# Summing expert rows into x on chip, spreading gate tiles, and moving a state copy in a hybrid decoder step

## The reference, cut to what matters

```python
x = x + (g_a * (y_a @ w_br_a) + g_b * (y_b @ w_br_b)) @ w_out     # RWKV-7 branch y_a, sparse attention branch y_b, gates g_a, g_b
x = x + moe_ffn(rms_norm(x, norm_ffn), ...)                       # top 4 of 32 experts per token
y = rms_norm(x, norm_final)

# moe_ffn, for every (token, expert) pair that the router chose
u   = h[token] @ w_up[e] + b_up[e]                                # w_up (32, 1024, 2048)
out = (min(u1, 7) * sigmoid(1.702 * u1) * (clip(u2, -7, 7) + 1)) @ w_down[e] + b_down[e]   # w_down (32, 1024, 1024)
result[token] += softmax_weight[token, e] * out
# and one of the outputs: new_win_kv_sample = the sample window state (8, 512, 2, 2, 64), moved on by one token
```

## Time and profile before

| what | value |
|---|---|
| median of the runs | 1611.16 us (1606.93 to 1612.17, 3 runs) |
| the profiled execution, its own time | 1601.41 us |
| its span, first to last instruction | 1599.6 us |
| mean granted PE clock | 0.952 |
| PE busy | 1341.8 us (84%) |
| DVE, ACT, POOL busy | 365.2, 201.3, 140.0 us |
| DMA, mean over the span | 488.81 MB, 306 GB/s |
| compress, attend_prompt, attend_samples begin | about 207, 293, 416 us |
| route, first_tiles, finish begin | about 533, 571, 1566 us |

### The profile page before, as it was taken

How to read it: one execution, slowest core, us unless ns; L and a number is a source line. 1 busy time by engine, 2 the same in 40 slices (tenths; PEclk the granted TensorE clock), 3 DMA queues, 4 the chain that set the end, 5 groups by cost and what they waited for, 6 DMA issues and landing times. The chain is left out here.

```text
span 1599.6 us, 21367 instructions
## 1 busy us (share of the span) xinstructions
PE 1341.8 (84%) x8262; PEld 665.5 (42%) x8263; DVE 365.2 (23%) x766; ACT 201.3 (13%) x432; POOL 140.0 (9%) x213
## 2 busy tenths in 40 slices
PE   6998889998889669988888888888888888888870
PEld 5887867786778523322222222222222222222220
DVE  2456473432341521101000100100010010001004
ACT  2221122122210201100000000000000000000001
POOL 1002040320000000000000000000000000000000
PEclk9999999899799669999999999999999999999995
DMA  5425083363272699999999999999999999999934
GB/s 168 129 84 136 4 242 124 108 234 149 106 197 66 240 366 417 417 416 415 418 418 415 418 418 416 416 418 417 415 418 418 415 416 418 416 415 417 418 135 150
DMA packets 142768, 488.81 MB, mean 306 GB/s; under 512 B 18926, under 2 KB 67296, under 8 KB 109328
## 3 DMA queue, kind: packets, MB, share of 16 engines
q1 hardware_dynamic: 131992, 457.55, 73.1%
q0 software_dynamic: 10320, 29.91, 5.2%
q10 hardware_dynamic: 400, 0.55, 0.1%
HBM read 483.57 MB, written 16.95 MB: 313 GB/s over the span
## 5 line engine op out<-in xcount | busy, mean ns | idle before, releaser
L2039 PE MATMUL bank<-ex_ring,ex_work 128*64 128x512 f32 x2048 | 492.2, 606 | 125.9 <-DMA ex_ring<-in_w_up 124.4
L2039 PEld LDWEIGHTS bank<-ex_ring,ex_work 128*64 128x64 f32 x2048 | 128.9, 137 | 466.0 <-DMA ex_ring<-in_w_up 280.0
L2057 PE MATMUL bank<-ex_ring,ex_work 128*64 128x512 f32 x1024 | 226.8, 595 | 0.7 <-ACT ex_work L1961 0.7
L1996 DVE TENSOR_SCALAR ex_work<-bank 128x512 f32<-128x512 f32 x32 | 22.1, 691 | 690.3 <-PE bank L2045 690.3
L2057 PEld LDWEIGHTS bank<-ex_ring,ex_work 128*64 128x64 f32 x1024 | 70.7, 137 | 134.0 <-issue 133.1
L498 PE MATMUL bank<-hT,w_group 128*128 128x264 f32 (+1 forms) x400 | 92.7, 394 | 0.7 <-DVE hT L398 0.7
L1941 POOL DMA_INDIRECT scratch_choice<-ex_work,ex_di x32 | 33.4, 1043 | 666.3 <-ACT ex_work L1971 666.3
L498 PEld LDWEIGHTS bank<-hT,w_group 128*128 128x128 f32 (+1 forms) x400 | 76.1, 191 | 16.6 <-DVE hT L398 1.1
L1293 PE MATMUL bank<-hT,w_cmp 128*128 128x264 f32 x256 | 68.2, 417 | 5.4 <-DMA w_cmp<-in_w_in 5.4
L1957 ACT ACTIVATE ex_work<-bank 128x512 f32<-128x512 f32 x33 | 19.7, 597 | 399.2 <-PE bank L2020 399.2
L2045 PE MATMUL bank<-ex_bias,ex_pick_up 32*64 32x512 f32 x256 | 61.8, 600 | 0.0
(11 more groups left out here) (464 smaller groups left out, 1229.4 us busy)
## 6 DMA issues: line engine op xcount, KB each, us to landing
ex_ring<-in_w_up SPq DMA_DIRECT2D x256, 1024.0 KB, 21.3
ex_ring<-in_w_down SPq DMA_DIRECT2D x256, 512.0 KB, 20.0
w_group<-in_w_in SPq DMA_DIRECT2D x12, 1024.0 KB, 5.4
w_cmp<-in_w_in SPq DMA_DIRECT2D x8, 1024.0 KB, 7.6
sel_rows<-in_w_out SPq DMA_DIRECT2D x8, 512.0 KB, 7.2
choice_rows<-scratch_choice SPq DMA_DIRECT2D x2, 2048.0 KB, 7.4
out_win_s<-in_state_win_kv POOLq DMA_DIRECT2D x1, 4088.0 KB, 24.9
x<-in_x_prompt SPq DMA_DIRECT2D x4, 512.0 KB
```

The costliest lines, as they stand in the source:

```text
L1996: nc.vector.tensor_scalar(g[:], banks[0][:], 7.0, None, ALU.min).then_inc(S["g_ready"], 1)
L2039: mm = mmul(banks[n // 2][lo:lo + SLOTS, :], B["xT"][:, k % 4, SLOTS * (k // 4):SLOTS * (k // 4) + SLOTS], B["ring"][:, k, 512 * n:512 * n ...
L2057: mm = mmul(banks[4][SLOTS * n:SLOTS * n + SLOTS, :], B["hT"][:, k % 4, SLOTS * (k // 4):SLOTS * (k // 4) + SLOTS], B["ring"][:, 8 + 4 * h ...
```

## The change

Three things change. (1) The experts' rows are no longer scattered to `choice` and read back. The routing table gives, for each slot, the token (as an odd number) and its weight, `slot_tw`; `dst_row` goes. For each expert DVE builds a *slot matrix* `back` (128 slots' halves by 384 tokens: the weight where slot and token meet, else zero), PE multiplies it with the result rows `y` (`comb`, 6 products of 64 rows by 128 by 512 columns, whose two halves of rows stand in different parts of the array), and DVE adds the 6 results to x (`adds`). `comb(e-2)` stands inside `up(e)` ahead of its third step. The stage `finish` goes; squares, root, scaling and the store follow in the block of `further_tiles`. The bias and pick tables are loaded twice, to partitions 0 to 31 and 32 to 63, and the 4 bias products of `up` are ordered and placed by it. (2) Gate tiles 12 to 15 are spread over units 8 to 15, half a tile per unit. (3) The copy of the window state is issued by POOL in `compress`, when the last cache piece has landed, instead of in `attend_prompt`.

```diff
@@ compress
                     for p in range(1, 8):
                         cmp_piece(pool, p)
+                    pool.wait_ge(C["raw_in"][7], 32)
+                    pool.dma_start(o["win_s"][0, :, 0:511]..., a["state_win_kv"][0, :, 1:512]...).then_inc(win_copied, 16)
@@ attend_prompt
+                tile_beside = [AHEAD + i if i < 8 else AHEAD + 8 + (i - 8) // 2 for i in range(16)]
-                    pool.wait_ge(mtd, 12)
-                    pool.dma_start(o["win_s"][0, :, 0:511]..., a["state_win_kv"][0, :, 1:512]...).then_inc(win_copied, 16)
-                        if 1 <= i <= NG - AHEAD:
-                            gate(AHEAD + i - 1)
+                        if i >= 1 and tile_beside[i - 1] != tile_beside[i]:
+                            gate(tile_beside[i - 1])
+                    gate(tile_beside[15])
-                        if i < NG - AHEAD:
-                            gate(AHEAD + i, 0, KD // 2)
+                        lo, n = (0, KD) if i < 8 else (KD // 2 * (i % 2), KD // 2)
+                        gate(tile_beside[i], lo, lo + n // 2)
                         turn(i)
-                        if i < NG - AHEAD:
-                            gate(AHEAD + i, KD // 2, KD)
+                        gate(tile_beside[i], lo + n // 2, lo + n)
@@ route, SP and DVE
-                    sp.dma_start(B["bias"][:, 0:2 * FF], a["b_up"][0]).then_inc(b_in, 16)
...
+                    for i in range(2):
+                        es = slice(NEXP * i, NEXP * i + NEXP)
+                        sp.dma_start(B["bias"][es, 0:2 * FF], a["b_up"][0]).then_inc(b_in, 16)
...
+                    step(nc.vector.memset(top_w[:], 0.0), top_ok)
+                    step(tt_(cell[:, :, :, 0, 0:NEXP], oh[:], dest[...], ALU.mult))
+                    dve.wait_ge(ex, 3)
+                    for t, (_, n) in enumerate(TILES):        # moved here from behind the table's cells
+                        step(nc.vector.reciprocal(tsum...))
+                        step(ts_(top_w..., tsum..., None, ALU.mult))
+                    step(tt_(cell[:, :, :, 1, 0:NEXP], oh[:], top_w[...], ALU.mult))
                     dve.wait_ge(rkd, 1)
...
+                    for t in range(3):
+                        step(ts_(B["iota"][:, P * t:P * t + P], num[:, 0:P], 2.0, float(2 * P * t + 1), ALU.mult, ALU.add))
@@ first_tiles, SP
+                    sp.dma_start(gain[:], bass.AP(a["norm_final"].tensor, 0, [[0, P], [1, D]])).then_inc(g_in, 16)
@@ first_tiles, POOL: scatter(e) is gone
@@ first_tiles, DVE
+                    def back(e):
+                        nc.vector.tensor_copy(B["tw"][:], slot_tw[:, bass.ds(e, 1), :]...)
+                        dve.wait_ge(S["tw_read"], e + 1)
+                        nc.vector.tensor_scalar(B["back"][:], B["iota"][:], B["tw"][:, 0:1], B["tw"][:, 1:2], ALU.is_equal, ALU.mult).then_inc(S["back_ready"], 1)
+                    def adds(e, wait, last):
+                        for i, (t, bank) in enumerate(last_banks if last else sum_banks):
+                            dve.wait_ge(S["comb"], 3 * e + i // 2 + 1)
+                            dst = x[0:n, t, 512 * (i % 2):512 * (i % 2) + 512]
+                            nc.vector.tensor_tensor(dst, banks[bank][0:n, :], dst, ALU.add).then_inc(S["added"], 1)
...
+                    with dve.Fori(3, NEXP) as e:
+                        adds(e - 2, True, False)
+                        back(e - 1)
                         tile(e, True)
@@ first_tiles, PE
+                    def comb(e, wait, last):
+                        pe.wait_ge(S["y_ready"], e + 1)
+                        pe.wait_ge(S["back_ready"], e + 1)
+                        for i, (t, bank) in enumerate(last_banks if last else sum_banks):
+                            hs = slice(SLOTS * (i % 2), SLOTS * (i % 2) + SLOTS)
+                            mm = mmul(banks[bank], B["back"][hs, P * t:P * t + P], B["y"][hs, :], start=True, stop=True)
+                            if i % 2:
+                                mm.then_inc(S["comb"], 1)
                         for k in range(KD):                                  # inside up(e)
+                            if back and k == 2:
+                                comb(e - 2, back > 1, False)
+                            if back and k == 4:
+                                pe.wait_ge(S["added"], 6 * (e - 2) + 1)
                             if wait and k == 4:
                                 turn_h(e - 1)
...
-                        for n in range(4):
-                            mm = mmul(banks[n // 2][lo:lo + SLOTS, :], B["pick_up"][:], B["bias"][:, 512 * n:512 * n + 512], ...)
+                        for n in (0, 2, 1, 3):
+                            lo, es = SLOTS * (n % 2), slice(NEXP * (n // 2), NEXP * (n // 2) + NEXP)
+                            mm = mmul(banks[n // 2][lo:lo + SLOTS, :], B["pick_up"][es, :], B["bias"][es, 512 * n:512 * n + 512], ...)
...
                     turn_h(NEXP - 1)
+                    comb(NEXP - 2, True, True)
                     down(NEXP - 1, NEXP // 2 - 1, 1, True)
+                    comb(NEXP - 1, True, True)
@@ further_tiles: each tile ends with comb and adds instead of a scatter; behind it, for everyone
+                    act: for each tile of x: Square with sum; later Sqrt
+                    dve: mean square; reciprocal; x * root * gain
+                    sp:  stores of y_p and y_s
@@ finish() and its read of scratch["choice"] are gone
```

More of the change, by code:

```diff
@@ L1688, in expert_buffers @@
             work = sb(moe, "ex_work", [P, 8, 512])
-            for name, shape, dt in (("ring", [P, 16, 2 * FF], F32), ("bias", [NEXP, 3 * FF], F32), ("pick", [NEXP, NEXP + 1], F32),
-                                    ("pick_up", [NEXP, SLOTS], F32), ("pick_down", [NEXP, SLOTS], F32),
-                                    ("si", [P, 1], U32), ("di", [P, 1], U32)):
+            for name, shape, dt in (("ring", [P, 16, 2 * FF], F32), ("bias", [2 * NEXP, 3 * FF], F32), ("pick", [2 * NEXP, NEXP + 1], F32),
+                                    ("pick_up", [2 * NEXP, SLOTS], F32), ("pick_down", [2 * NEXP, SLOTS], F32),
+                                    ("si", [P, 1], U32), ("tw", [P, 2], F32), ("iota", [P, 3 * P], F32), ("back", [P, 3 * P], F32)):
                 B[name] = sb(moe, "ex_" + name, shape, dt)
@@ L2006, in tile @@
                             dve.wait_ge(S["down_done"], e)
-                            nc.vector.tensor_copy(B["pick_down"][:], B["pick"][:, bass.ds(e, 1)].to_broadcast([NEXP, SLOTS])).then_inc(S["pick_down"], 1)
+                            nc.vector.tensor_copy(B["pick_down"][:], B["pick"][:, bass.ds(e, 1)].to_broadcast([2 * NEXP, SLOTS])).then_inc(S["pick_down"], 1)
+                    back(0)
                     tile(0, False)
-                    with dve.Fori(1, NEXP) as e:
+                    tile(1, True)
+                    adds(0, False, False)
+                    back(1)
+                    tile(2, True)
+                    with dve.Fori(3, NEXP) as e:
+                        adds(e - 2, True, False)
+                        back(e - 1)
                         tile(e, True)
+                    adds(NEXP - 2, True, True)
+                    back(NEXP - 1)
+                    adds(NEXP - 1, True, True)
+                    dve.wait_ge(S["added"], 6 * NEXP)
                 @block.tensor
@@ L2015, in _, with turn_x @@
                     mmul = nc.tensor.matmul
-                    def turn_x(e):
+                    def turn_x(e, back=False):
                         pe.wait_ge(S["x_in"], 16 * (e + 1))
+                        if back:
+                            pe.wait_ge(S["added"], 6 * (e - 2))
                         for k in range(4):
@@ L2080, in _ @@
                     turn_h(NEXP - 1)
+                    comb(NEXP - 2, True, True)
                     down(NEXP - 1, NEXP // 2 - 1, 1, True)
+                    comb(NEXP - 1, True, True)
         def further_tiles(B):
-            names = ("w", "x_in", "x_turned", "xT", "up", "g", "lin", "sig", "l", "h", "h_turned", "hT", "down", "y_ready", "y_out", "idx", "pick")
+            names = ("w", "x_in", "x_turned", "xT", "up", "g", "lin", "sig", "l", "h", "h_turned", "hT", "down", "y_ready", "comb", "idx", "pick", "tw", "back", "added")
             w_in, x_in, x_turned, xT_ready, up_done, g_ready, lin_ready, sig_ready, l_ok, h_ready, h_turned, hT_ready, \
-                down_done, y_ready, y_out, idx, pick_ok = (sem("more_" + n) for n in names)
+                down_done, y_ready, comb_ok, idx, pick_ok, tw_read, back_ok, added = (sem("more_" + n) for n in names)
             ring, y = B["ring"], B["y"]
+            sums = ((0, 2), (0, 3), (1, 5), (1, 6), (2, 7), (2, 0))
+            sq_out = ring[:, 0, 0:D]
+            ss = sb(moe, "final_ss", [P, 3])
+            sq, ms, root, y_ok = (sem("fin_" + n) for n in ("squares", "ms", "root", "y_ready"))
+            x_ok = Signal("fin_x_ready")
             def each(eng, tile):
```

(30 more changed lines are left out.)

180 lines of the change are left out of this document (72 added, 108 removed).

## The result

| | before | after |
|---|---|---|
| median | 1609.41 us (1606.93 to 1612.17, 4 runs) | 1551.20 us (1547.17 to 1552.77, 4 runs) |
| ratio | | 0.9649, 95% interval 0.9627 to 0.9671 |
| profiled execution: span, mean PE clock | 1599.6 us, 0.952 | 1545.4 us, 0.956 |

A forecast was written before the change was run, and what follows sets the result against it. The prediction took DMA to bound the experts' stage, PE's order of work and single waits the stages ahead. Terms -10.5 + 0 + 21 - 15 - 19 = -23.5 us, from 1611.2 to 1587.7 us; range 1566 to 1600.

The forecast's parts named there:

- The loop, -10.5: Experts' loop: the scatter's share of DMA engine time goes, 10.5 us less; low end of the gain zero.
- What goes is the scatter: Experts' loop: the transfers lose only the scatter, 3.65 of 333.4 MB, 1.1% of the time; 10.5 us less.
- `comb` hidden: Experts' loop: PE's added 2.9 us per expert, 26.9 to 29.8, hides under transfers of 30.5 us; cost 0.
- PE becomes the bound: Rival, experts' loop: PE needs 32.4 us per expert, loop +47 instead of -10.5, time 1645; chance 0.05.
- decides from 3.6 us added per expert on: Experts' loop: PE work added per expert beyond which PE is the bound, from 30.5 - 26.9.
- Route, 0: Route stage: moved weight steps, index tiles and doubled bias and pick loads cost 0, bounds -0.5 and +2.
- The copy, +21: Compress: the copy holds back SP's rows, PE waits for `ys`; +21 us, bounds 0 and +24.
- it hurts little: Rival, copy in compress: cost 0 to 8 us instead of 21, time about 1570; chance 0.2.
- attend_prompt, -14: Units 8 to 15: no 5.40 us wait for gate weights, clock kept up; -14 us, bounds -8 and -17.
- The end, -19: After the experts: `finish` goes, `comb` and adds come; -19 us in all, bounds -16 and -21.
- `comb(31)` and the adds need 0.9 + 4.1 = 5.0: +1: The end, after the last `y`: these replace a scatter of some 4 us, costing 1 us more.
- One block boundary less, -0.5: The end: without `finish` one block boundary goes, 0.5 us less.

The follow-up runs named there:

- the gate run: Kernel after, with one gate tile beside each of units 0 to 11 and none beside 12 to 15, copy still in compress: 1562.57 us, ratio 0.9721.

## Why the prediction was wrong, point by point

- **The loop, -10.5: failed, measured -29.1.** The step that failed is "What goes is the scatter", taken as all that changes for the transfers. 16 us are the ring's address, a side effect of a table that takes 192 bytes more; six kernels show it. No view of the profile of before shows an address, but the sizes of the buffers ahead of the ring are in the code, and the rule of the Trainium skill quoted above, though it tells of reads, would have raised the question. The scatter itself was mis-sized too: 13.3 us (its run alone) for 10.5, and where the other 2.8 come from is open.
- **`comb` hidden: right, by a wrong count.** The 2.6 us per `comb` were right. The 26.9 us of PE's need were 25.1. I took the period less the named waits, 3.9 us on the average of 32 experts, and this expert waited 4.4; and PE's busy time holds waiting too. The kernel before, an expert with a full ring and the one of the earlier trace rows, the same 117 instructions:

```profile
617.20:642.30 25.10, 25.10 (x117) 8.14 (x118) 2.94 (x6) 2.31 (x4) 2.47 (x4) 1.00 1.02 414
1005.30:1036.14 30.84, 26.48 (x117) 7.67 (x118) 2.94 (x7) 2.31 (x4) 2.47 (x4) 1.00 1.02 417
```

The first experts, which find the ring full, show the need directly. The rival "PE becomes the bound" was priced rightly in kind, but "decides from 3.6 us added per expert on" should be 29.6 - 25.1 = 4.5 us: at 4.7 added PE was the bound and the loop lost 5 us, at 7.2 it lost 82.
- **Route, 0: right** (-0.9, inside what executions differ by).
- **The copy, +21: right in place and mechanism, +18.0 in size.** The rows landed at 272.4 for the 274 forecast, the copy at 265.0 for 265. The rival that it hurts little (0.2) is out. The rule of the Trainium skill on packet turns (same page, section on queues, rings and completion order), by the estimate in the prediction, would have given 15; the turns measured are 30 packets of SP's for 30 of the copy's, one for one, where the page has 9 to 17 descriptors a turn. The size is 3 us off because the rows landed 7.4 us behind the copy for the 9 forecast, and because the stretch itself begins 1.5 us later than before.
- **attend_prompt, -14: right** (-14.5), and its two causes were borne out by the gate run: 7.6 us by the spreading, 6.9 by the copy's going. That the size fits is luck in part: the wait for the gate weights, 5.40 us in the profile of before, is 10.2 and 7.5 us in the traces of the two other kernels that leave this stage as it was (the one with 192 bytes more, the one without scatters). The next stage gained 2.7 for the 1 forecast.
- **The end, -19: mis-sized, -26.3.** `comb(30)` cost 2.3 (2.0 forecast), `finish` gave 21.2 (21.1). Two steps failed. "`comb(31)` and the adds need 0.9 + 4.1 = 5.0: +1" was -3.7 (9.7 us to the engines' meeting before, 6.0 after): I took the landing of the scatter for the end of its cost, and behind it POOL drained for 5.37 us. Without scatters it is 2.76, and the whole stretch 6.4 us shorter. "One block boundary less, -0.5" was -3.6: the boundary held everybody until PE had branched; in the trace of the run that puts one back it costs 3.2, which that run's time alone can't tell.

The signs of the terms were right, and their order was not: the loop, forecast as the smallest of the four large terms, is the largest. Two gains were too small, for the greater part because of effects outside the instructions that the diff names.

## What to carry to other kernels

Ask of every change what it does to the addresses of the large DMA targets behind it: with a ring that takes the DMA engines' whole time, 64 bytes cost 15 us of 1550, and a pad costs no time. Read an engine's need per round where it is not held up (the first rounds on a full ring), not as period less named waits. A big copy between DRAM and DRAM in few rows held up the small transfers beside it, so put such a copy behind the last small transfer that someone waits for; and count at a block's end the drains and the branches of engines that have nothing to do.

## What the runs showed of the hardware

- Weight rows that land 64 or 128 bytes past a multiple of 256 take 314.0 instead of 309.1 ns (8 KB) and 162.7 to 162.9 instead of 159.0 (4 KB). On a multiple, the 8 KB packets of 640 to 1440 us from the 1st to the 99th percentile all take 309 (kernel after, and the ring 256 further); off it they spread from 309 to 325 (the ring alone 64 further) or to 331 (everything 64 further).
- A copy of 8 rows of 511 KB from DRAM to DRAM, beside small transfers of another queue: 30 small packets pass with 30 of 65 KB. Two issues on that queue stood for 20.16 us, until the copy had landed.
- Eight instructions of 32 rows by 64 columns of the array, placed in two row groups and two column groups, take 1.09 us, against 1.93 in two column groups alone.
- POOL's drain took 5.37 us behind an indirect store that had landed, 7.61 with an indirect load just issued, and 2.76 where the last one had been issued 38 us before; PE's branch over a skipped block takes 3.3 to 4.0 us over the runs here, DVE's 0.07.
- In a loop whose transfers alone take 29.6 us per expert over its length (30.0 in the middle), a PE need of 27.2 us costs nothing, 29.75 costs 5 us in 910, and 32.3 costs 82: each time what PE's need is over the 29.6.
